# Two unsplit weight units a pair instead of four, one one-hot matrix for gather and scales, and part of the hidden vector's work moved to ScalarE

## What is computed

```python
return (jax.nn.silu(xb @ w1[e]) * (xb @ w3[e])) @ w2[e]
...
out = jnp.einsum('nkd,nk->nd', y.reshape(n_tok, TOP_K, d), e_w.astype(y.dtype))
```

## Time and profile before

| | |
|---|---|
| median of 3 runs | 2151.68 us (2151.1 to 2153.07) |
| the profiled execution's own time | 2152.64 us |
| its span, first to last instruction | 2150.8 us |
| PE busy / DVE busy / ACT busy | 2106.5 / 1552.3 / 1187.2 us |
| mean granted TensorE clock | 0.994 |
| the experts' part | from about 1098 us of the span to its end |

### The profile page before, as it was taken

The page is one execution under the profiler, slowest core; times in us unless marked ns, Lnnn a source line. Parts: engine busy times, 40 slices in busy tenths (PEclk is TensorE's granted clock), DMA queues, the critical chain, the costliest instruction groups (busy, mean ns, idle before and its releaser), DMA issues.

```text
span 2150.8 us, 29080 instructions
## 1 busy us (share of the span) xinstructions
PE 2106.5 (98%) x11430; PEld 1749.5 (81%) x11430; DVE 1552.3 (72%) x1480; ACT 1187.2 (55%) x967; POOL 105.0 (5%) x76
## 2 busy tenths in 40 slices
PE   8999999999999999998999999999999999999996
PEld 8998888899999998887887777777777777777774
DVE  7656664453737365545668899998989998999898
ACT  5445663333333323333346777777777777777783
POOL 1000000000000000001000000000000000000010
PEclk9999999999999999999999999999999999999998
DMA  6554335655454445668667999999999999999994
GB/s 213 157 151 159 118 122 177 202 189 162 156 175 151 162 156 176 208 204 261 233 256 304 412 412 412 416 410 413 414 406 418 408 411 411 408 412 413 409 419 185
DMA packets 140958, 606.45 MB, mean 282 GB/s; under 512 B 17179, under 2 KB 29611, under 8 KB 114379
## 3 DMA queue, kind: packets, MB, share of 16 engines
q1 hardware_dynamic: 137328, 597.99, 73.4%
q0 software_dynamic: 3552, 7.37, 1.1%
HBM read 595.05 MB, written 22.04 MB: 287 GB/s over the span
## 4 chain that ended last, share of the span: by engine, by line
PE 89%; DVE 4%; issue 3%; ACT 2%; DMA 1%; POOLq 0%; POOL 0%; DVEq 0%; ACTq 0%
PE ps L1954 18%; PE ps L1935 15%; PE ps L1090 12%; PE ps L1091 12%; PE ps L1087 10%; PE ps L1072 5%; PE ps L2312 4%; PE ps L1112 2%; PE ps L2067 2%; PE ps L2027 1%; PE ps L2040 1%; DVE wl L760 1%; DVE wl L1509 1%; PE ps L1115 1%; PE ps L2199 0%
## 5 line engine op out<-in xcount | busy, mean ns | idle before, releaser
L760 DVE TENSOR_TENSOR wl<-raw,wh 128x2048 fp32r<-128x2048 f32 x319 | 716.4, 2287 | 86.7 <-ACT wh L606 85.7
L606 ACT ACTIVATE wh<-raw 128x2048 fp32r<-128x2048 f32 x319 | 598.0, 1911 | 202.8 <-PE ps L1091 131.2
L1509 DVE TENSOR_TENSOR wl<-raw,wh 128x2048 fp32r<-128x2048 f32 (+1 forms) x168 | 379.9, 2263 | 286.2 <-ACT wh L1311 286.1
L1311 ACT ACTIVATE wh<-raw 128x2048 fp32r<-128x2048 f32 (+1 forms) x168 | 317.9, 1895 | 448.1 <-DMA raw<-in_w_in_dram 279.5
L1090 PE MATMUL ps<-wh,xg 128*128 128x512 f32 x888 | 366.2, 412 | 1.9 <-DVE wl L760 1.9
L1091 PE MATMUL ps<-wl,xg 128*128 128x512 f32 x888 | 347.5, 391 | 0.0
L1935 PE MATMUL ps<-hth,wh 128*128 128x272 f32 (+1 forms) x896 | 259.8, 290 | 3.2 <-DVE wl L1509 1.8
L1935 PE MATMUL ps<-htl,wh 128*128 128x272 f32 (+1 forms) x896 | 255.7, 285 | 0.0
L1935 PE MATMUL ps<-hth,wl 128*128 128x272 f32 (+1 forms) x896 | 255.6, 285 | 0.0
L1090 PEld LDWEIGHTS ps<-wh,xg 128*128 128x128 f32 x888 | 167.6, 189 | 42.7 <-issue 10.2
L1091 PEld LDWEIGHTS ps<-wl,xg 128*128 128x128 f32 x888 | 167.5, 189 | 39.8 <-issue 7.7
(11 more groups left out here) (361 smaller groups left out, 3004.8 us busy)
## 6 DMA issues: line engine op xcount, KB each, us to landing
raw<-in_w_dram SPq DMA_DIRECT2D x192, 2048.0 KB, 10.0
raw<-in_w_in_dram SPq DMA_DIRECT2D x103, 1024.0 KB, 5.0
raw<-in_w_pa_dram SPq DMA_DIRECT2D x16, 1024.0 KB, 5.0
raw<-in_w_pb_dram SPq DMA_DIRECT2D x16, 1024.0 KB, 5.0
raw<-in_w_out_dram SPq DMA_DIRECT2D x16, 1024.0 KB, 5.1
raw<-in_w_ukv_dram SPq DMA_DIRECT2D x8, 1024.0 KB, 5.3
yscr<-zeros SPq DMA_DIRECT2D x4, 1024.0 KB, 8.3
yrow<-yscr SPq DMA_DIRECT2D x4, 1024.0 KB, 12.9
```

The costliest lines, as they stand in the source:

```text
L606: nc.scalar.activation(wh2[:, x % HELD, :], raw_of(turn, x), ACT.Copy).then_inc(s_wh2, 1)
L760: nc.vector.tensor_tensor(wl_of(turn, x), raw_of(turn, x), wh2[:, x % HELD, :].bitcast(F32), ALU.subtract).then_inc(s_wl2, 1)
L1311: nc.scalar.activation(wh[:, n % RING1, 0:c], raw1[:, n % RING1, 0:c], ACT.Copy).then_inc(s_wh, 1)
L1509: nc.vector.tensor_tensor(wl[:, n % RING1, 0:c], raw1[:, n % RING1, 0:c], wh[:, n % RING1, 0:c].bitcast(F32), ALU.subtract).then_inc(s_wl, 1)
```

## The change

- `XR` becomes (10, 22): two unsplit units in 24, at steps 14 and 2. Unit 0 of the run is split too. So the first pair, up to unit 19, has one unsplit unit instead of five.
- The opening is reordered for that: ACT splits units 0, 1 and 2 before it copies the router's logits (that copy moves behind them), and DVE does `lo` of units 0 to 3 one by one between the first four `gathered_rest`.
- One matrix `pd`, with two buffers, is built by `gather_matrix` and serves the gathers and the scales; `pg` is gone and `select` only copies eight weights. The tile `hv` moves to another place.
- The activation is Silu instead of Sigmoid, so `product` has one multiplication instead of two.
- The rounding of the hidden vector (`hidden_hi`) is done by ACT, one step after the activation; DVE's remaining subtraction also moves one step on.
- Gathers follow steps 4, 8, 15 and 17 instead of 4, 8, 16 and 20.

```diff
-        XR = (1, 7, 13, 19)
+        XR = (10, 22)
...
-        hv = place("hv", [P, KF, SLOTS], M0 + 5120)
+        hv = place("hv", [P, KF, SLOTS], K0 + 1536)
...
-        pg = place("pg", [P, TT, 2 * SLOTS], M0 + 5120 + 1024)
-        pd = place("pd", [P, TT, 2, 2 * SLOTS], M0 + 7168)
+        pd = place("pd", [P, 2, TT, 2, 2 * SLOTS], M0 + 5120)
...
-            return x % 24 in XR or (isinstance(turn, int) and 24 * turn + x == 0)
+            return x % 24 in XR
...
-        G_AT = (4, 8, 16, 20)
+        G_AT = (4, 8, 15, 17)
...
-        G_FIRST = (8, 10, 16, 20)
+        G_FIRST = (8, 10, 16, 18)
...
-                nc.scalar.activation(sg[:, :], ps[:, 6, 0:4 * SLOTS], ACT.Sigmoid).then_inc(s_sg, 1)
+                nc.scalar.activation(sg[:, :], ps[:, 6, 0:4 * SLOTS], ACT.Silu).then_inc(s_sg, 1)
+
+            def hidden_hi(j, to=hx):
+
+                act.wait_ge(s_hp, j + 1)
+                nc.scalar.activation(to[:, :, 0:SLOTS], hv[:, :, :], ACT.Copy).then_inc(s_hxh, 1)
...
                     if k == 14 and early:
                         sigmoid(2 * turn)
+                        hidden_hi(2 * turn)
+                    if k == 1 and not first:
+                        hidden_hi(2 * turn - 1)
+                    if k == 13 and not early:
+                        hidden_hi(2 * turn)
...
-            hi(0, 2)
+            for x in range(3):
+                hi(0, x)
+            act.wait_ge(s_lgt, 1)
+            nc.scalar.activation(lgt[:, :], ps[0:N_GROUPS + N_EXP, 0, 0:SEQ], ACT.Copy).then_inc(s_lgc, 1)
...
+            def gather_matrix(g, col, par):
+
+                need(dve, s_hm, 2 * (g - 1) if not isinstance(g, int) or g else 0)
+                slots = slots2[:, :].unsqueeze(1).unsqueeze(1).broadcast_to([P, TT, 2, 2 * SLOTS])
+                ranks = rk_[:, :, bass.ds(col, 2)].unsqueeze(3).broadcast_to([P, TT, 2, 2 * SLOTS])
+                nc.vector.tensor_tensor(pd[:, par, :, :, :], slots, ranks, ALU.is_equal).then_inc(s_pg, 1)
...
-            for q in range(2):
+            nc.vector.tensor_reduce(rs[:, 18:19], r2[:, :, :].rearrange("p t e -> p (t e)"), AXX, ALU.max).then_inc(s_mxr, 1)
+            for q in range(GQ):
+                lo(0, q)
                 gathered_rest(0, 0, q, FIRST_BANK[q])
-            nc.vector.tensor_reduce(rs[:, 18:19], r2[:, :, :].rearrange("p t e -> p (t e)"), AXX, ALU.max).then_inc(s_mxr, 1)
-            lo(0, 2)
-            for q in range(2, GQ):
-                gathered_rest(0, 0, q, FIRST_BANK[q])
-            lo(0, 3)
...
-                nc.vector.tensor_tensor(pd[:, :, :, :], slots, ranks, ALU.is_equal)
                 nc.vector.tensor_copy(wdc[:, :, :, :], wd[:, :, bass.ds(2 * p, 2), :]).then_inc(s_pd, 1)
...
-                nc.vector.tensor_tensor(hv[:, :, :], a, sg[:, :].rearrange("p (f s) -> p f s", f=KF),
-                                        ALU.mult).then_inc(s_ha, 1)
...
-                nc.vector.tensor_tensor(hv[:, :, :], hv[:, :, :], b, ALU.mult).then_inc(s_hp, 1)
+                nc.vector.tensor_tensor(hv[:, :, :], b, sg[:, :].rearrange("p (f s) -> p f s", f=KF),
+                                        ALU.mult).then_inc(s_hp, 1)
...
-                nc.vector.tensor_scalar_mul(to[:, :, 0:SLOTS], hv[:, :, :], 1.0).then_inc(s_hxh, 1)
...
+                    if k == 1 and not first:
+                        hidden_split(2 * turn - 1)
+                    if k == 13 and not early:
+                        hidden_split(2 * turn)
                     if k == 1 and not first and not last:
-                        gather_matrix(turn + 1, 2 * p + 2)
+                        gather_matrix(turn + 1, 2 * p + 2, 1 - par)
```

More of the change, by code:

```diff
@@ L601, in hi @@
                 landed2(act, turn, x)
-                if isinstance(turn, int) and 24 * turn + x <= HELD:
+                if isinstance(turn, int) and 24 * turn + x < HELD:
                     act.wait_ge(s_wused, N_UNITS)
@@ L653, in pair @@
                         copy_up(turn, x, 2 * turn + 1, 1)
-                    if x + HELD != HELD or not early:
-                        hi(turn, x + HELD)
+                    hi(turn, x + HELD)
                     if k == 14 and early:
                         sigmoid(2 * turn)
+                        hidden_hi(2 * turn)
[3 more added lines that the diff above has]
+                        hidden_hi(2 * turn)
                     if k == 9 and early:
@@ L673, in pair @@
                         sigmoid(2 * turn + 1)
+                        hidden_hi(2 * turn + 1, hx2)
                     if k == 10 and last:
@@ L939, in pair @@
                     if k == 13 and early:
-                        hidden(2 * turn, 0, turn)
+                        product(2 * turn, 0, turn)
+                        hidden_split(2 * turn)
                     lo(turn, x + HELD)
@@ L944, in pair @@
                     if k == 0 and not first:
-                        hidden(2 * turn - 1, 1, turn - 1)
+                        product(2 * turn - 1, 1, turn - 1)
+                    if k == 1 and not first:
+                        hidden_split(2 * turn - 1)
+                    if k == 13 and not early:
+                        hidden_split(2 * turn)
                     if k == 1 and not first and not last:
-                        gather_matrix(turn + 1, 2 * p + 2)
+                        gather_matrix(turn + 1, 2 * p + 2, 1 - par)
                     for q in range(GQ):
@@ L959, in one_round @@
                 if not early:
-                    gather_matrix(turn, 0)
+                    gather_matrix(turn, 0, 0)
                     for q in range(GQ):
@@ L1058, in tensor_experts, with gather @@
             nc.tensor.matmul(ps[:, 7, 0:N_EXP], before[:, :], asg[:, 1, :], start=False, stop=True).then_inc(s_rank, 1)
-            def gather(g, q, *waits):
+            def gather(g, q, par, *waits):
                 pe.wait_ge(s_pg, g + 1)
@@ L1100, in down, with mix @@
                 unit(turn, x, [(ps[:, banks[nb], :], of[:, c, :], 512 * nb) for nb in range(4)], c == 0, c == 3)
-            def mix(turn, j, a, *waits):
+            def mix(turn, j, a, par, *waits):
                 pe.wait_ge(s_ac, j + 1)
@@ L1114, in mix @@
                 for t in range(TT):
-                    m = nc.tensor.matmul(ps[:, 7, 0:2], pd[:, t, a, :], wdc[:, t, a, :], start=t == 0, stop=t == 1,
+                    m = nc.tensor.matmul(ps[:, 7, 0:2], pd[:, par, t, a, :], wdc[:, t, a, :], start=t == 0, stop=t == 1,
                                          skip_group_check=True)
@@ L1157, in pair @@
                     if early and k < 2:
-                        gather_blocks(2 + k, FIRST_BANK[2 + k])
+                        gather_blocks(2 + k, FIRST_BANK[2 + k], 0)
                     if k == 0 and not first:
-                        mix(turn - 1, j - 1, 1)
+                        mix(turn - 1, j - 1, 1, 1 - par)
                     if k == (14 if early else 12):
-                        mix(turn, j, 0, *([(s_hp, j), (s_stc, rounds)] if last else [(s_xgl, GQ * (turn + 1) + 2)]))
+                        mix(turn, j, 0, par, *([(s_hp, j), (s_stc, rounds)] if last else [(s_xgl, GQ * (turn + 1) + 2)]))
                     if k == 20 and last:
-                        mix(turn, j + 1, 1, (s_hp, j + 1))
+                        mix(turn, j + 1, 1, par, (s_hp, j + 1))
                     if k == 8 and last:
@@ L1174, in pair @@
                         if k == (G_FIRST if first else G_AT)[q] and not last:
-                            gather(turn + 1, q, (s_hp, j if q < 2 else j + 1))
+                            gather(turn + 1, q, 1 - par, (s_hp, j if q < 2 else j + 1))
             def stream_back(t):
@@ L1191, in one_round @@
                     for q in range(GQ):
-                        gather(turn, q)
+                        gather(turn, q, 0)
                 pair(turn, 0, first=True, early=early)
@@ L1495, in _ @@
                 turned(j)
-            act.wait_ge(s_lgt, 1)
-            nc.scalar.activation(lgt[:, :], ps[0:N_GROUPS + N_EXP, 0, 0:SEQ], ACT.Copy).then_inc(s_lgc, 1)
             scalar_experts(act)
```

31 lines of the change are left out of this document (7 added, 24 removed).

## The result

| | before | after |
|---|---|---|
| median (lowest to highest), us | 2152.14 (2151.1 to 2153.07), 4 runs | 2179.69 (2174.68 to 2183.74), 4 runs |
| profiled execution, its span | 2152.64, 2150.8 | 2176.99, 2174.9 |
| mean granted clock, profiled run | 0.994 | 0.985 |

The changed kernel takes 1.0127 times the time of the kernel before (95% interval 1.0102 to 1.0152): it is 27.6 us slower, where 2172 was predicted. Its four runs spread over 9 us, the four of before over 2, and the spread follows the clock: 2174.68 us at a mean granted clock of 0.986, 2176.99 at 0.985, 2182.4 and 2183.74 at 0.982.

A forecast was written before the change was run, and what follows sets the result against it. PE was taken to set the pace, with DVE and the transfers close behind. From 2152.6: opening -5.0, pairs +5.6, their clock +14.3, last pair +4.2, its clock +1.0, giving 2172.7; median forecast 2172, range 2126 to 2184 us.

The forecast's parts named there:

- opening: the next pair's first unit: Before the steady pairs, the next pair's first unit was to begin at 1181.8 instead of 1186.8 us, a saving of 5.0.
- a pair without a spell: A steady pair of experts with no stretch at 1.2 GHz: 62.2 us against 61.8, +5.6 us over 14 pairs.
- PE's idle time a pair, and before step 12: PE idle about 2.2 us before each pair's first unit, released by DVE's `lo`, and about 0.9 before step 12.
- last pair without a spell: Last pair: ACT's copy to `xn` delays `hi`, so PE waits 6.6 us before unit 12; +4.2 us net, low clock excluded.
- clock in the 14 pairs: A 1.2 GHz stretch costing 1.7 us after PE's 2.2 us idle time, in six of ten pairs: +14.3 us.
- clock in the last pair: One 1.2 GHz stretch in the last pair, at the same six in ten: +1.0 us.
- all of the clock: Total cost of 1.2 GHz stretches, in the 14 pairs and the last pair: 15.3 us.
- The ring: `hi` waits for PE to finish the unit four before, so DVE can't run ahead; PE stalls 1.1 and 2.5 us a pair.
- The waits come, the clock holds: Rival: PE's waits appear in the pairs but cost no clock, 2156.4 us; chance 0.15.
- The clock falls in every pair: Rival: a 1.2 GHz stretch of 1.7 us follows PE's idle time in all pairs, 2182 us; chance 0.10.
- Faster, ACT and DVE keep up, 2116: Rival: PE doesn't wait for the split; pairs of 59.7 us give 2116, transfer-bound 61.2 gives 2136; no or small waits 0.25.
- Records of the granted clock at half in most pairs: Expected sign in the profile after: PE's granted clock at half in most pairs, with a pair of 63.9 us where it falls.

## Why the prediction was right, and what it missed

The direction and the mechanism were right, and the time was 7.7 us under the measured one. By its own steps, from the profiled executions (+24.35 us) and, for the clock, from the runs:

| step | predicted | measured | from |
|---|---|---|---|
| opening: the next pair's first unit | 1181.8, -5.0 | 1182.18, -4.1 | timeline, first records |
| a pair without a spell | 62.2, +5.6 in 14 | 62.12, +4.3 | pair starts |
| PE's idle time a pair, and before step 12 | 2.2 and 0.9 | 2.18 and 0.77 | timeline |
| last pair without a spell | +4.2 | about +2.6 | start to end, less spells |
| clock in the 14 pairs | +14.3, 8.4 spells of 1.7 | +14.6 to 14.9, 5 spells | starts less 62.12 each |
| clock in the last pair | +1.0 | about +6.4, 2 spells | the two spells' lengths |
| all of the clock | 15.3 | 23.0, with the spell left there some 24 to 25 | median less the filled wait's |

**A reading of the earlier trace rows.** They show the second record of each pair's first unit, not the first. The first ones are (the opening's end, the last pair):

```profile
1186.28 0.79 PE L1090 MATMUL ps<-wh,xg 128*128 128x512 f32 x1
...
2051.66 0.79 PE L1090 MATMUL ps<-wh,xg 128*128 128x512 f32 x1
```

The pair stays at 61.81 us. But the next pair began at 1186.28 and not at 1186.8, so the opening is 4.1 us shorter, where 5.0 was predicted. In the same way the first record behind an unsplit unit starts 0.63 us before the second and not 0.23, so 3.44 us is the unsplit unit with 0.4 of delay that shows up behind it. The sums by pair are untouched. The terms without the clock add up to +2.8 us, where +4.8 was predicted.

**The ring.** PE's saving of 3.3 us a pair turned into waiting, nearly to the microsecond, and released by the records that the walk names. Two experiments move the cause and the wait goes with it: `output_rest` behind a `lo` (a pair of 59.67) or a free step of DVE where it stands (61.04). Putting four unsplit units back removes it altogether. That this stretch, and not the merged matrix, Silu or the rounding, makes the time, the unchanged 2153.51 us with four unsplit units shows.

**The term that was mis-sized: the clock spells.** "A spell costs 3.5 x 0.49 = 1.7 us" and "six in ten" were both off, in opposite directions, and in the 14 pairs of the profiled run they cancel. Only 5 of 14 starts are followed by a spell. Three of these are 3.4 us long and cost 1.6 (a pair of 63.7). Two are 10.2 us long and cost 4.8 (a pair of 66.95); the 10.25 us window above is one. In it the mix, 16 records of 64 columns, takes 3.51 us, against 1.89 in a pair without a spell. In the last pair one of each came, where one of 1.7 was expected at six in ten. In the medians the clock makes 23.0 us or somewhat more instead of 15.3. That is the 7.7 us missing, and the 2 us by which the other terms were too long went the other way. So the closeness of the 14 pairs' clock term (+14.3 against +14.6 to 14.9) is luck: too many spells at too low a price. A second small step failed with it: the median was taken 1.0 us *below* the profiled run as before, but with spells that come by chance the profiled run is a draw, here 2.7 us below the median.

The Trainium skill ("TensorE: Matmul & The Clock Gate", section "Why this matters for your kernels") warns of idle gaps longer than these, and by its rule the term would be zero. The runs disagree: idle times of 2.2 to 2.7 us cost 23.0 us here. What the earlier trace rows showed at 1.86 us before was no single accident either: the kernel before with moved outputs has the same 1.86 us in its opening, and the low clock behind it.

**The rivals.** *The waits come, the clock holds*, put at 2156.4, was built by filling the wait and measured 2156.66. One short spell is still in that, so the price of all that isn't clock was right within about 2 us, and the 0.3 us between the two numbers is closer than the terms were. *The clock falls in every pair* has the wrong count, 5 and not 14, although the median, 2179.7, is near its 2182; its size comes from the long spells. *Faster, ACT and DVE keep up, 2116* did not happen, since `output_rest` stood in the way, but moving it gave 2119.66 and 2115.97. So the price of that case came out, with the outputs moved, and its bound by transfers (61.2 us a pair at 411 GB/s) was wrong: they gave 427. The 433 GB/s of the earlier trace rows was not the best short window of before, as the prediction has it: one of 5 us (1180 to 1185) reads 449. The Trainium skill's ceiling of 435 GB/s ("DMA: Bandwidth & Descriptors", "Where 436 GB/s comes from") lies above the windows of 100 us and more here, 411 to 427, but not above all of 3 to 6 us, in which up to 449 were read.

**Small steps.** The moved rounding holds nobody up, as said, and saves nothing either, until DVE is the bound. `pd` in two buffers and Silu cost nothing that four unsplit units would show. "Records of the granted clock at half in most pairs" did not come: it was 5 of 14.

## What to carry to other kernels

When two engines share a split in order, through a ring of a few places, sums of busy time don't tell whether it keeps up. Walk the stretch between the points where the slower engine catches up, and put its other work where it has a free step; here one place further on was worth 60 us. Price an idle time of PE of about 2 us not at its length but at its length plus the slow stretch that may follow, and watch for stretches as long as 10 us. When a fill leaves part of a wait, look in the trace which waits the spells stand behind before the cost is put down to the one that was changed. When such a wait can't be removed, filling it with matmuls that nobody reads is an experiment that separates the two prices, and by itself gave 23 us back here.

## What was not expected of the hardware

- Behind the same wait of 2.2 to 2.7 us the clock did one of three things in one execution: it held (9 pairs' starts of 14), fell for 3.4 us (3, and one in the last pair), or fell for 10.2 (2, and one in the last pair). Read from the spacing of PE's records, the fall came 0.7 to 1.1 us after PE's restart where it lasted 3.4, and 1.2 to 1.4 after it where it lasted 10.2. The profile with the rounding back on DVE (four long, two short) and the last or first pairs of the other variants (one long, five short) keep that order: all 11 short falls behind such waits came by 1.15 us after the restart, all 8 long ones later. The later a fall, the more of its start lies on the thin matmuls of the mix. That these make it long is argued and was not tested.
- No idle time of 1.80 us or less was followed by the low clock in any kept profile, 12 of the 29 between 2.16 and 2.33 us were, and 7 of the 10 near 2.7. How likely it is between 1.80 and 2.16, three cases don't tell.
- The transfers ran at 427 GB/s in a steady 100 us, with PE, DVE and ACT 99%, 98% and 84% busy, 16 GB/s more than the same queue moved before.
